# Second attention reordered, layer norm's sums moved to GpSimd and VectorE, first up unit reordered, last tile finished by halves

## The reference

```python
def conv_ffn(h, w_up, conv_w, conv_b, w_down, valid):
    up = jnp.einsum('bld,df->blf', h, w_up)
    a, b = jnp.split(up, 2, axis=-1)
    ...
def attend(qn, qr, kn, kr, v):
    s = jnp.einsum('bqhd,bkhd->bhqk', qn, kn) + jnp.einsum('bqhd,bkd->bhqk', qr, kr)
    p = jax.nn.softmax(s.astype(jnp.float32) * ATTN_SCALE, axis=-1).astype(v.dtype)
    return jnp.einsum('bhqk,bkhd->bqhd', p, v)

def conformer_conv(u, conv_w, conv_b, ln_g, ln_b, w_pw):
    a, g = jnp.split(u, 2, axis=-1)
    y = a * jax.nn.sigmoid(g)
    y = lax.conv_general_dilated(y, ...) + conv_b      # depthwise, 31 taps
    y = jax.nn.silu(layer_norm(y, ln_g, ln_b))
    return y @ w_pw

def peer_ffn(h, w_pq, sub_keys, u_tab, v_tab):
        ...
        act = jax.nn.gelu(jnp.einsum('thkd,td->thk', u_tab[expert], xc), approximate=False)
        return jnp.einsum('thk,thkd->td', gate * act, v_tab[expert])
```

## Time and profile before

| what | value |
|---|---|
| median of three runs | 2880.2 us |
| the profiled execution | 2883.77 us, of it the span 2882.5 us |
| TensorE busy | 2560.6 us (89%) |
| VectorE busy | 1706.4 us (59%) |
| GpSimd busy | 666.4 us (23%) |
| ScalarE busy | 648.0 us (22%) |
| HBM traffic, mean | 238 GB/s; about 420 GB/s in the expert layer |

### The profile page before, as it was taken

The page is one execution under the profiler, slowest core; times in us unless marked ns, Lnnn a source line. Parts: engine busy times, 40 slices in busy tenths (PEclk is TensorE's granted clock), DMA queues, the critical chain, the costliest instruction groups (busy, mean ns, idle before and its releaser), DMA issues.

```text
span 2882.5 us, 24291 instructions
## 1 busy us (share of the span) xinstructions
PE 2560.6 (89%) x8314; PEld 1398.8 (49%) x8314; DVE 1706.4 (59%) x3694; ACT 648.0 (22%) x1584; POOL 666.4 (23%) x567
## 2 busy tenths in 40 slices
PE   8998989999999999999999989799877777777776
PEld 5655458887444444466665544355422323232222
DVE  1132459986127982366545676867575767667554
ACT  2222220001020002366412211322121221222112
POOL 0000022441000000000002334444443444444331
PEclk9999999999999999999999999999999999999999
DMA  4101123443222121000249999999999999999996
GB/s 158 59 30 59 46 77 150 159 175 147 102 82 96 62 78 51 15 1 30 81 150 358 406 396 404 419 417 420 420 420 420 420 420 420 420 420 420 420 420 287
DMA packets 87305, 687.01 MB, mean 238 GB/s; under 512 B 9976, under 2 KB 10616, under 8 KB 12816
## 3 DMA queue, kind: packets, MB, share of 16 engines
q0 software_dynamic: 73728, 536.90, 45.3%
q1 hardware_dynamic: 12016, 143.99, 13.0%
q10 hardware_dynamic: 1440, 4.57, 0.4%
HBM read 683.32 MB, written 2.10 MB: 238 GB/s over the span
## 4 chain that ended last, share of the span: by engine, by line
PE 47%; DMA 26%; DVE 5%; ACT 2%; issue 1%; POOL 1%; ACTq 0%; DVEq 0%; POOLq 0%
PE psum L398 21%; DMA weights<-in_experts,expert 13%; PE psum L1102 12%; DMA slot<-in_experts,expert 8%; DMA xn<-in_experts,expert 5%; PE psum L908 3%; PE psum L998 3%; PE psum L860 2%; PE psum L976 2%; PE psum L930 2%; PE psum L966 1%; PE psum L916 1%; DVE slot L2210 1%; DVE weights L2210 1%; ACT spare_row L1551 1%
## 5 line engine op out<-in xcount | busy, mean ns | idle before, releaser
L1102 PE MATMUL psum<-slot,spare_row 128*128 128x512 f32 x872 | 413.0, 618 | 93.9 <-ACT spare_row L1551 93.7
L1102 PE MATMUL psum<-weights,spare_row 128*128 128x512 f32 x848 | 392.9, 607 | 114.0 <-ACT spare_row L1551 111.9
L2280 POOL DMA_INDIRECT slot<-in_experts,expert x218 | 232.8, 1068 | 665.5 <-PE psum L1102 337.3
L2210 DVE CUSTOM_DVE_ANT_0 slot<-slot,hT 128x1024 f32<-128x1024 f32 x218 | 265.2, 1222 | 160.4 <-DMA slot<-in_experts,expert 159.4
L2210 DVE CUSTOM_DVE_ANT_0 weights<-weights,hT 128x1024 f32<-128x1024 f32 x212 | 258.3, 1223 | 146.8 <-DMA weights<-in_experts,expert 145.6
L1102 PEld LDWEIGHTS psum<-weights,spare_row 128*128 128x128 f32 x848 | 155.4, 191 | 339.0 <-ACT spare_row L1551 177.5
L1102 PEld LDWEIGHTS psum<-slot,spare_row 128*128 128x128 f32 x872 | 164.8, 195 | 316.8 <-issue 170.4
L2280 POOL DMA_INDIRECT weights<-in_experts,expert x212 | 224.5, 1059 | 317.8 <-PE psum L1102 312.0
L1546 ACT ACTIVATE coef<-hidden 128x2 f32<-128x2 f32 (+1 forms) x257 | 52.2, 203 | 984.8 <-DVE hidden L2210 984.8
L398 PE MATMUL psum<-hT,weights 128*128 128x512 f32 (+1 forms) x576 | 249.7, 596 | 1.9 <-ACT hT L1142 1.9
L398 PE MATMUL psum<-xnT,weights 128*128 128x264 f32 (+1 forms) x1040 | 244.1, 389 | 8.2 <-DVE gT L1798 2.9
(11 more groups left out here) (347 smaller groups left out, 3279.5 us busy)
## 6 DMA issues: line engine op xcount, KB each, us to landing
weights<-in_w_mod SPq DMA_DIRECT2D x12, 2048.0 KB, 8.4
weights<-in_w_up SPq DMA_DIRECT2D x11, 2048.0 KB, 7.8
weights<-in_w_in SPq DMA_DIRECT2D x8, 2048.0 KB, 8.3
weights<-in_w_pq SPq DMA_DIRECT2D x8, 2048.0 KB, 10.9
weights<-in_w_out SPq DMA_DIRECT2D x6, 2048.0 KB, 9.2
weights<-in_w_in_t SPq DMA_DIRECT2D x4, 2048.0 KB, 7.5
weights<-in_w_down SPq DMA_DIRECT2D x4, 2048.0 KB, 8.4
weights<-in_w_o_mla SPq DMA_DIRECT2D x4, 2048.0 KB, 10.5
```

The costliest lines, as they stand in the source:

```text
L1102: last = pe.matmul(acc.pair[:, half, :], k.diags[pick % 8], k.slots[slot][:, D + half * 512:D + (half + 1) * 512], start=h0 == 0 and j == ...
L2210: ins = dve.tensor_tensor_reduce(slot[:, 0:D], slot[:, 0:D], k.h2[:, i, :], 1.0, 0.0, ALU.mult, ALU.add, hid[:, j:j + 1])
L2280: pool.indirect_dma_start(k.slots[slot], None, k.A["experts"], bass.IndirectOffsetOnAxis(ap=k.expert[b % 2][:, j:j + 1], axis=0))\
```

## The change

Four edits:

1. In the first up unit, product 2 of h = 0 moves from behind product 7 to behind product 1, ahead of the last tile's transposes; product 7 waits for three input sums rather than four, and product 4 waits for the fourth.
2. For the mean, GpSimd adds the eight channel groups into one (seven additions, each as its convolution ends) and TensorE does one matmul with ones. For the variance, VectorE adds the eight squares in between its subtractions (seven additions), and again TensorE does one matmul. The mean stands in a buffer of its own. TensorE's order becomes: latents 0, 1 and 2, `ln_mean`, rotary keys, `ln_sq`, gates.
3. In the second attention the first queries come ahead of `values2`, each `q_rope` comes ahead of its two `q`, and the weighted values come one step later (c = 8, 12, ...).
4. The last tile is finished by halves: after the first half's last matmul VectorE multiplies and adds the first 512 columns, then the second. ScalarE loads the root's table ahead of that and squares by halves; VectorE multiplies by the gain while ScalarE finds the root, so that a scaling by one number is what is left.

The core of the diff:

```diff
@@ ffn_up, tensor program @@
                 product((u_, 0, 1), left(blocks[0], 0), low_left)
+                product((u_, 0, 2), left(blocks[1], 0), high_left)
                 turn2(3)
                 product((u_, 1, 1), left(blocks[0], 1), low_left)
...
                 if u_ == 0:
-                    pe.wait_ge(s.up_xsum, 4)
+                    pe.wait_ge(s.up_xsum, 3)
                 product((u_, h, 7), left(blocks[2], h), t3, reads=2)
-                product((u_, h, 2), left(blocks[1], h), high_left)
+                if u_ or h:
+                    product((u_, h, 2), left(blocks[1], h), high_left)
                 pe.wait_ge(s.up_sum, 4 * u_ + 4)
                 product((u_, h, 3), left(sums[2], h), high_right)
+                if u_ == 0:
+                    pe.wait_ge(s.up_xsum, 4)
                 u = product((u_, h, 4), left(blocks[3], h), t4)
@@ latents_and_norm, tensor program @@
         latent(1)
+        latent(2)
         u = take("ln_mean")
-        pe.wait_ge(s.conv, KC)
-        chain(u.pair[:, 0, :], [(k.ones[:], k.merged[:, n, :]) for n in range(KC)]).then_inc(u.fill())
-        latent(2)
-        u = take("ln_sq")
-        for n in range(KC):
-            pe.wait_ge(s.ln_sq, n + 1)
-            pe.matmul(u.pair[:, 0, :], k.ones[:], k.sg[n % 3][:], start=n == 0, stop=n == KC - 1).then_inc(u.fill())
+        pe.wait_ge(s.conv_sum, KC - 1)
+        pe.matmul(u.pair[:, 0, :], k.ones[:], k.ln_sum, start=True, stop=True).then_inc(u.fill())
         u = rope_keys("kr_x", w, k.hT, SEQ)
         k.ring_done[unit] = u.full[-1]
+        u = take("ln_sq")
+        pe.wait_ge(s.ln_sq_sum, KC - 1)
+        pe.matmul(u.pair[:, 0, :], k.ones[:], k.ln_sum, start=True, stop=True).then_inc(u.fill())
         gates(3)
@@ layer_norm, vector program @@
-        for n in range(KC):
-            dve.tensor_tensor(k.merged[:, n, :], k.merged[:, n, :], k.sg[2][:], ALU.subtract).then_inc(s.centred)
+        for n in range(KC + 2):
+            if n < KC:
+                dve.tensor_tensor(k.merged[:, n, :], k.merged[:, n, :], k.ln_mean, ALU.subtract).then_inc(s.centred)
+            if n > 2:
+                dve.wait_ge(s.ln_sq, n - 1)
+                if n > 3:
+                    dve.wait_ge(s.ln_sq_sum, n - 3)
+                dve.tensor_tensor(k.ln_sum, k.sg[0][:] if n == 3 else k.ln_sum, k.sg[(n - 2) % 3][:], ALU.add).then_inc(s.ln_sq_sum)
@@ GpSimd program @@
+    for n in range(1, KC):
+        pool.wait_ge(s.conv, n + 1)
+        if n > 1:
+            pool.wait_ge(s.conv_sum, n - 1)
+        pool.tensor_tensor(k.ln_sum, k.merged[:, 0, :] if n == 1 else k.ln_sum, k.merged[:, n, :], ALU.add).then_inc(s.conv_sum)
@@ attention, tensor program @@
-            if c >= 4 and c % 4 == 3:
-                u = values((c - 4) // 8, (c - 4) // 4 % 2)
+            if c >= 8 and c % 4 == 0:
+                u = values((c - 8) // 8, (c - 8) // 4 % 2)
@@ peer, tensor program @@
                     for half in range(2):
+                        if half and pick == len(k.gathers) - 1:
+                            last.then_inc(s.half_picked)
@@ new: finish_last, vector program @@
+        dve.wait_ge(s.ld_final2, 16)
+        for half in range(2):
+            cut = slice(half * 512, (half + 1) * 512)
+            if half == 0:
+                dve.wait_ge(s.half_picked, 1)
+            else:
+                dve.wait_ge(s.picked, NT * PH * TOPK)
+            dve.tensor_tensor(y[:, cut], u.pair[:, half, :], k.g2[:, cut], ALU.mult).then_inc(v.up())
+            dve.wait_ge(*v.now())
+            dve.tensor_tensor(k.x[:, i, cut], k.x[:, i, cut], y[:, cut], ALU.add).then_inc(s.x5)
+        dve.wait_ge(s.x5, NT + 1)
+        dve.tensor_tensor(y, k.x[:, i, :], k.final[:], ALU.mult).then_inc(v.up())
+        r = inverse(P, i, ("last", i))
+        dve.tensor_scalar(y, y, r, None, ALU.mult).then_inc(s.y)
```

More of the change, by code:

```diff
@@ L333, in memory @@
     k.sg = [at(f"sg{i}", 26664 + SEQ * i, [P, SEQ]) for i in range(3)]
+    k.ln_sum, k.ln_mean = (k.scratch2[:, i * SEQ:(i + 1) * SEQ] for i in range(2))
     k.sig_a = k.xn2[:].rearrange("p i (a n) -> p (i a) n", n=SEQ)
@@ L1428, in attention @@
         queries(0)
+        act.wait_ge(*of["pw", KC - 1].free)
+        values2()
         keys(0)
@@ L2019, in attention @@
         queries(0)
-        for c in range(AH * NT + 4):
+        for c in range(AH * NT + 5):
             if c < AH * NT:
```

84 lines of the change are left out of this document (51 added, 33 removed).

## The result

The changed kernel's median is 2857.65 us in four runs (2849.99 to 2861.16), against 2882.56 in four runs of the kernel before (2877.77 to 2889.76). The ratio is 0.9909, with a 95% interval of 0.9891 to 0.9926: 0.9% faster. The forecast was 2858.1, in a range of 2850 to 2867, worked out from the 2880.2 of the first three runs; the fourth run of the kernel before moved its median up by 2.4.

What follows compares the result with a forecast made beforehand. Before the first gather at 1506 us TensorE's work and waits count, after the last matmul only the tail. Gains 1.5 + 7.1 + 11.1 + 2.4 = 22.1 us from the 2880.2 median give 2858.1, range 2850 to 2867.

Steps and rivals of the forecast that it cites:

- "a few microseconds" of waits in the second attention: Second attention: TensorE's waits in the whole of it were put at a few microseconds, TensorE doing nearly everything there.
- Rival (c): Expert layer: gathers bound by something that does not move with their start, only the tail's 2.4 counts, 2878 us; chance 0.04.
- Edit 1, 1.5 us: First up unit: product 2 moved ahead and product 7 waiting for the third sum only gain 1.4 to 1.7 us, taken as 1.5.
- The idle 5.17 us stays: First up unit: TensorE's 5.17 us wait for the second input sum remains, and products 6 and 5 start near 406.2.
- Edit 2, 7.1 us: Layer norm: gates start 9.5 us earlier, less 2.0 for clock and 0.4 for the mean, giving 7.1, bounds 5.5 and 9.8.
- the price of GpSimd's additions: Convolution: each GpSimd addition costs VectorE 0.84 of its time, so five delay the convolution by 4 to 6 us.
- Edit 3, 11.1 us: Second attention: start 2.2 plus clock 1.9, later `q_swap` 2.5, later weighted values 4.5, giving 11.1, bounds 8.5 and 12.3.
- Edit 4, 2.4 us: Tail: halves and the table load out of the chain shorten last matmul to store by 2.4 us, bounds 2.0 and 2.6.
- Rival (a): Layer norm and scores: clock falls in both new gaps, VectorE's chain 2 us longer, scores start slow; 2865 to 2871; chance 0.09.
- Rival (b): Layer norm and scores: the clock holds in both places, 2.0 and 1.1 us more gained, 2855 us; chance 0.05.
- Rival (d): Convolution: slower if a GpSimd addition costs over 4.4 us in the chain; at 5 us each, 2885; chance 0.02.
- The signs named beforehand: First gather near 1486, 3 to 4 us idle and clock 0.50 at `ln_sq`, two wait signs, under 4.6 us to the store.

Runs made afterwards that it cites:

- `ln_vec`: The changed kernel with the mean's seven additions on VectorE behind the convolution instead of on GpSimd beside it; median 2860.45 us, ratio 0.9915 to before.
- `ln_twice`: The changed kernel with each of GpSimd's seven additions for the mean done twice; median 2861.46 us, ratio 0.9919 to before.
- `up_pool`: The changed kernel with GpSimd's sums for the second up unit held back until VectorE's four input sums are done; median 2856.65 us, ratio 0.9905 to before.

## Why the prediction was right, point by point

**What bounds the kernel.** Right, though "a few microseconds" of waits in the second attention was too low: those ahead of the queries, the scores and the values add up to 12.4. The gathers' stage, from the first gather to the store, took 1370.7 us against 1373.6, and in all thirteen profiles 1366.9 to 1373.6. It moved with its start. Rival (c), the gathers absorbing the gain, falls.

**Edit 1, 1.5 us.** The size holds (1.6 on average, 1.65 at the same clock), and so does the working. The chain is delayed by product 2: with the clock as before, product 6 starts 19.1 us behind the metadata transposes in `ln_vec` and 17.3 before, the 1.75 forecast. In the profiled pair the delay isn't seen, because the half clock lay over the transposes there. "The idle 5.17 us stays" was true, but I did not ask what made it so long. My sentence that GpSimd's sums for unit 1 lie long ahead of their use was right on the use and overlooked whom they stand beside: they more than double VectorE's sums. That was the largest thing open in this place, 3.5 us.

**Edit 2, 7.1 us; measured 8.4.** Removed 13.3 and the new idle time of 3.40 (3.7 forecast) are as worked out. The step that failed is the price of GpSimd's additions. I took 0.84 of their time, 4 to 6 us for five, from a row in which VectorE's operand was in SBUF. They cost 2.0: the convolution ended 1.55 us ahead of latent 1's end before, and 0.44 behind it after, and was itself 2.0 longer. `ln_twice` shows that the price is about right for an addition that meets SBUF operations only (0.9, against 1.07 by the 0.84), and the channels' lengths show that of the five only the last is such a one (0.96). The others stand wholly or partly beside multiplications out of PSUM and cost 0 to 0.57. So TensorE didn't wait for the mean (0.4 was counted). The clock took 1.7, and 2.0 was counted.

The Trainium skill's rule in "SBUF — State Buffer", section "SBUF: two separate sides", is that the pair of ports is held for a whole instruction and the other engine blocks. The traces agree, 3.3 us for each of two overlapping sums; it is where the 6 us for five additions came from. For VectorE the section limits it to operations with two inputs in SBUF or in a two-port mode, and beside the multiplications out of PSUM the additions did cost nothing; whether the scalings that were slowed run in such a mode, no trace here shows. The rule of the "GPSIMD Engine Reference", section "4.1 Engine selection", that additions belong on VectorE, would have done as well: `ln_vec` gives the same stretch.

**Edit 3, 11.1 us; measured 11.9.** The start gave 3.6 (4.1 counted). The 1.8 us of idle time for the keys is as forecast, but the clock fell behind it all the same in this profile: 16 rows took 7.09 (5.40 at full clock), against 8.77 before, so 1.7 of the 1.9 counted came. The full-clock length had been put at 6.24 at most; it is 5.40, so that a start without a fall gives 3.4, more than the bound of 3. The wait for the next keys' copies grew from 0.37 to 0.64 us. The later `q_swap` gave 3.2 (2.5 counted), the later values 5.1 (4.5). Both terms left out what a wait costs beside its idle time, 0.25 us each for the `q_swap` and 0.07 for the values.

**Edit 4, 2.4 us; measured 2.7.** Within its bounds, by the mechanism described. The squares of the second half ended at 2855.84, 2.82 behind the last matmul's end (2.9 forecast).

**The sum.** 22.1 was forecast and 22.7 came in the profiled pair, but the agreement is partly luck. The edited stretches gave 24.5, and the unedited ones took back 2.0 in this pair of profiles. The medians agree by luck too: 2857.65 lies 0.5 below the forecast of 2858.1, but they differ by 24.9 (21 to 31 by the ratio's interval), and taking 22.1 from the before's median of four runs would give 2860.5. So the edits were priced some 2 to 3 us too low in sum, mostly edit 2 (1.3) and edit 3 (0.8), and the base stood 2.4 too low. Rival (a) asked for longer gaps and a fall behind both; the falls came, the longer gaps did not. Rival (b), no fall in either place, did not occur: in the layer norm all eight profiles with the gap of 3.40 us lost 1.4 us or more, while at the scores four of eight with the gap of 1.80 kept the clock. Rival (d) would need 4.4 us for an addition, and the five cost 0.4 on average and 0.96 at most. The signs named beforehand came: the first gather at 1486.49, the idle time and the low clock at `ln_sq`, no wait for `q_rope`'s copy, one wait of 1.0 for the values, 4.15 us to the store.

## What to carry to other kernels

Before taking an idle time as given, look at what the two engines that share SBUF ports do in it: holding back work that isn't due can halve the sums that everybody waits for. In this kernel a wait removed was worth its idle time, 0.07 to 0.25 us beside it, and often 1.7 us of half clock behind it (in four profiles of eight behind 1.80 us, in all eight behind 3.40); independent work moved into the gap earns all three. And split the span at fixed events: a stretch without an edit shows how much of a difference is only the phase of the clock.

## What the hardware showed that I had not expected

The first 387 us, the same instructions in all thirteen profiles, took 386.9 to 387.1 (four kernels), 388.8 to 389.1 (three), 392.0 to 392.5 (five) or 394.5 us, up to 7.6 us apart, which is more than edits 1 and 4 together. The granted clock over them falls with it (0.99 for 0 to 387 us in the kernel before, 0.98 in the changed one, 0.97 in `up_pool`). Runs of one kernel differ by 4 to 16 us, and this is of the same size. Read in short windows, the clock took 5.1 us from the stretch in the first seven kernels, 8.5 in the next five and 10.2 in `up_pool`. What is left is 381.8 to 384.3 us, so the clock explains some 5 of the 7.6. The remaining 2.5, the step from 387 to 389 above all, may come from whether a fall meets idle time, where it costs nothing; that is not shown.

Whether GpSimd's addition slows VectorE depends on the operand: a VectorE multiplication out of PSUM was not slowed by it (0.69 us with it), a scaling of 512 columns in SBUF was, from 0.54 to 1.12, and sums over 1028 columns from 1.23 to 3.37. So an addition beside the convolution cost anything from 0 to 0.96 us, by the place where it fell.
